# A hybrid attention layer on eight cores: value projections set among query and key projections, gates and cumulative sums moved into the projection stage

## The chip, the cores and the metric

One Trainium2 chip, eight cores. Each core runs the same program on one of the eight batch elements; no core sends anything to another. The time is the device time of the slowest core in microseconds (us). A core has a matrix engine (TensorE, PE in the rows; PEld is its weight load), a vector engine (VectorE, DVE), an activation engine (ScalarE, ACT), GpSimd (POOL) and SyncE (SP). Each engine takes its instructions strictly in program order; POOL and SP also issue DMA transfers, in the same order as their other work.

## The reference, cut

```python
hn = rms_norm(x, g_mix) * (1.0 + sc1) + sh1
proj = hn @ w_in                                  # 2048 x 3080
mq, mk, mv, fq, fk, fv, f_logit = jnp.split(proj, offs, axis=-1)   # six of 512 columns, 8 logits
mq = partial_rope(rms_norm(mq per head, moba_q_gain), positions)   # 8 heads of 64, rope on 16
mk = partial_rope(rms_norm(mk per head, moba_k_gain), positions)
fq = rms_norm(fq per head, fox_q_gain); fk = rms_norm(fk per head, fox_k_gain)
log_f = jax.nn.log_sigmoid(f_logit + b_forget)
# MoBA: blocks of 256 keys; a query keeps its own block and the top 3 past blocks
gate = einsum('bhtd,bhnd->bhtn', mq, mean of mk over each block)
# FoX: softmax(q k / 8 + cum[q] - cum[k]), cum = cumsum(log_f), causal
x = x + gt1 * (concat(o_moba, o_fox) @ w_out)
hn = rms_norm(x, g_ffn) * (1.0 + sc2) + sh2
x = x + gt2 * (swiglu(causal conv of width 3 over hn @ w_up) @ w_down)
```

## The kernel before

A sequence has 2048 tokens, 16 tiles of 128. The program is one list of operations per engine. `Prog` records each operation in program order and derives the waits from the bytes that it reads and writes, and for PSUM from the bank; the engines then run their own lists. So the order in which Python emits the work is the order on each engine, and an engine waits for its next instruction even if a later one could go.

The stages are: normalise and transpose x into `hnT` (T1), project it and prepare heads (T2), attention for 16 heads (T3), output projection and second norm (T4), the channel sub-layer (T5). The change lies in T2.

T2 works in units (line 600). A unit is one group of columns for one tile: `pe_unit(n)` does eight accumulating matmuls of 128x512 into PSUM bank `n % 4`. `groups` gives the order mq, mk, mv, fq, fk, fv, fl, each over 16 tiles: 112 units. The loop at line 674 is a software pipeline: iteration n emits `pe_unit(n)`, then `stage_a(n-1)`, `stage_b(n-4)` and `stage_a2(n-2)`.

- For mq, mk, fq and fk, `stage_a` squares the bank on ACT, sums per head on DVE (line 632) and takes the root on ACT. `stage_a2` takes the reciprocal on DVE (line 644) and multiplies the bank by it on DVE, which frees the bank.
- `stage_b` applies the gains on POOL. For mq and mk POOL first writes the 16 rope columns (128x128) and then the other 48 per head (128x384), and four DVE operations do the rope on the first product.
- For mv and fv, `stage_a` is one ACT copy from the bank and nothing else. For fl (8 columns) it is one small DVE addition.

Weights come as 512-column pieces into two alternating buffers `wch`, each piece issued by POOL when the group before it starts (line 607). Eight pieces of the adaLN weights (`late_pieces`) come through one buffer `wlate`: the transfer is issued at units 2, 14, 26, ... and PE uses the piece eight units later, the first four as 32 matmuls of one column, the last four as 8 of 512.

After the loop, lines 689 to 746 run with no projection beside them: `make_ab`; exp and log of the forget logits on ACT; two f32 matmuls that sum within and over tiles; a chain of 15 additions on DVE for the prefix over tiles; the splitting of the sum into three bf16 columns of FQ and FK; 112 one-column matmuls for the block means of the keys; and for tiles 8 to 15 the gate: eight PE transposes, a DVE copy, eight small matmuls, a DVE copy, a comparison, a reduction and the mask columns of MQ. T3 starts with POOL's memsets of `vaug` (which lies in the bytes of `hnT`), the transposes of head 0 (line 784), 16 warm-up matmuls and the first scores, whose exp is the first ACT work of T3.

Of the kernel before, what the change touches and what calls it, by code (L numbers as in the profile page):

```python
# [256 lines left out]
def build_program(debug=False, stop_after=None):  # L257
# [435 lines left out]
    act(zf, zf, AF.Ln, bias=one_ap, scale=1.0)  # L693
    ts("dve", zf, zf, -1.0, None, ALU.mult)
    pbc = pbank(4)
    mm(pbc[:, 0:128], tri_f, zf, True, True)
    pbt = pbank(5)
    mm(pbt[:, 0:128], ones_f, zf, True, True)
    copy("dve", totb, pbt[:, 0:128])
    pref3 = pref.rearrange("p (i h) -> p i h", i=NT)  # L700
    tot3 = totb.rearrange("p (i h) -> p i h", i=NT)
    memset("dve", pref3[:, 0, :], 0.0)
    for i in range(1, NT):
        tt("dve", pref3[:, i, :], pref3[:, i - 1, :], tot3[:, i - 1, :], ALU.add)
    tt("dve", cum, pbc[:, 0:128], pref, ALU.add)
    ts("dve", negcum, cum, -1.0, None, ALU.mult)
    cum3 = cum.rearrange("p (i h) -> p i h", i=NT)
    r3 = res1.rearrange("p (i h) -> p i h", i=NT)
    copy("dve", FQ[:, :, :, 64], cum3)
    tt("dve", r3, cum3, FQ[:, :, :, 64], ALU.subtract)  # L710
    copy("dve", FQ[:, :, :, 65], r3)
    tt("dve", r3, r3, FQ[:, :, :, 65], ALU.subtract)
    copy("dve", FQ[:, :, :, 66], r3)
    for q_ in range(3):
        ts("dve", FK[:, :, :, 67 + q_], FQ[:, :, :, 64 + q_], -1.0, None, ALU.mult)
# [2 lines left out]
    kmT3 = kmT.rearrange("p (h n) -> p h n", h=8)
    pbk = pbank(6)
    for h in range(H):  # L720
        for n in range(7):
            for s in range(2):
                mm(pbk[0:64, h * 8 + n: h * 8 + n + 1], MK[:, 2 * n + s, h, 0:64], invc[:, 0:1], s == 0, s == 1)
    memset("dve", kmT[0:64, :], 0.0)
    for h in range(H):
        copy("dve", kmT3[0:64, h, 0:7], pbk[0:64, h * 8: h * 8 + 7])
    for i in range(8, NT):
        b = i // 2
        sl = i % 2
        pbt_ = pbank_bf(5)  # L730
        for h in range(H):
            tr(pbt_[0:64, h * 128:(h + 1) * 128], MQ[:, i, h, 0:64], ident_b)
        copy("dve", qt0[sl][0:64], pbt_[0:64, 0:1024].rearrange("p (h q) -> p h q", h=8))
        pbg = pbank(7)
        for h in range(H):
            mm(pbg[:, h * 8:(h + 1) * 8], qt0[sl][0:64, h, :], kmT3[0:64, h, :], True, True)
        copy("dve", gate_s[sl], pbg[:, 0:64])
        g3 = gate_s[sl].rearrange("p (h n) -> p h n", h=8)
        cmp4 = cmp_s[:, 0:8 * b * b].rearrange("p (h n m) -> p h n m", h=8, n=b)
        in0 = g3[:, :, 0:b].unsqueeze(2).to_broadcast([128, 8, b, b])  # L740
        in1 = g3[:, :, 0:b].unsqueeze(3).to_broadcast([128, 8, b, b])
        tt("dve", cmp4, in0, in1, ALU.is_gt)
        rk = rank_s[:, 0:8 * b].rearrange("p (h n) -> p h n", h=8)
        P.op("dve", (lambda o, a: (lambda e: e.tensor_reduce(out=o, in_=a, axis=AX.X, op=ALU.add)))(rk, cmp4),
             reads=[cmp4], writes=[rk])
        ts("dve", MQ[:, i, :, 64:64 + b], rk, 3.0, NEG, ALU.is_ge, ALU.mult)
# [343 lines left out]
```

How the kernel before makes its waits and increments, by code:

```python
        def run_engine(ename, eng):  # L203
            seen = {}
            for o in prog.ops[ename]:
                waits = {}
                for d in o.deps:
                    key, sem, val = sem_of(d)
                    if seen.get(key, 0) >= val:
                        continue
                    if key not in waits or waits[key][1] < val:
                        waits[key] = (sem, val)
                if o.is_dma:
                    e, j = o.dma_sem
                    key = ("d", e, j)
                    pv = o.dma_val - 16
                    if pv > 0 and seen.get(key, 0) < pv:
                        if key not in waits or waits[key][1] < pv:
                            waits[key] = (dsems[e][j], pv)
                for key, (sem, val) in waits.items():
                    eng.wait_ge(sem, val)
                    seen[key] = val
                ins = o.fn(eng)
                if o.is_dma:
                    e, j = o.dma_sem
                    ins.then_inc(dsems[e][j], 16)
                elif o.signal:
                    ep = (o.sig_idx - 1) // SEM_EPOCH
                    ins.then_inc(esems[ename][ep], 1)
            if ename in dsems:
                for j, s in enumerate(dsems[ename]):
                    if dcount[ename][j] > 0:
                        eng.wait_ge(s, dcount[ename][j])
```

## Time and profile before

| | |
|---|---|
| median of 3 runs | 1477.72 us (1476.7 to 1493.68) |
| the profiled execution | 1477.1 us |
| its span, slowest core (6) | 1475.5 us; the eight cores 1465.8 to 1475.5 us |
| mean granted TensorE clock | 0.95 on each core |
| busy over the span | PE 81%, DVE 63%, ACT 51%, POOL 17% |
| chain that ended last | PE 45%, DVE 26%, issue 13%, ACT 7%, DMA 5% |

Busy shares are means over stages with different limits. A stretch of the trace shows which engine is full in it, and the idle time in brackets behind a row shows what ended the wait. The clock is given in parts of the full 2.4 GHz; 0.5 is the 1.2 GHz level, and a stretch in between is a mean over both. A matmul's time includes its way through the engine: eight in a row of 128x512 show 1.89 us, but follow one another at 1.73 us per eight.

### The profile page before, as it was taken

The page shows a single profiled execution, that of the slowest core. Times are in us where ns is not written, and L with a number is a line of the kernel's source. Part 1 is how long each engine was busy: PE and PEld are TensorE (multiplying, and loading weights), DVE is VectorE, ACT ScalarE, POOL GpSimd, SP SyncE. Part 2 cuts the span into 40 slices and gives each one's busy share as a digit, 9 for nine tenths or more (in the row PEclk, how much of TensorE's full clock was granted, in tenths as well). Part 3 has the DMA queues.
Part 4 walks back from the last instruction along what each step waited for, and adds up shares of the span by engine and source line. Part 5 has one row for each costly group of instructions (what it writes and reads, how often), then busy time and mean ns, then how long its engine had stood idle before and what let it go on. Part 6 is the DMA issues. An engine that isn't in the chain of part 4 may idle for free.

```text
span 1475.5 us, 21224 instructions; the slowest of 8 cores (1465.8 to 1475.5 us)
## 1 busy us (share of the span) xinstructions
PE 1199.8 (81%) x6516; PEld 573.3 (39%) x6516; DVE 925.6 (63%) x1420; ACT 748.8 (51%) x1212; POOL 243.9 (17%) x224
## 2 busy tenths in 40 slices
PE   0086569995799999889999894589997989989888
PEld 0052224444444444434444343434443434434333
DVE  3508883726466666666666535578748865875885
ACT  1062223330488888768888402567416732751770
POOL 1014440331000000230000000023202320330330
PEclk9999999995799999989999996899999999999999
DMA  9851345430000001110000440122112112121105
GB/s 226 160 67 28 49 61 83 70 46 2 1 1 2 1 1 30 44 44 1 1 1 15 123 149 1 34 67 43 30 58 57 29 29 72 29 43 43 30 15 228
DMA packets 34557, 74.32 MB, mean 50 GB/s; under 512 B 2960, under 2 KB 21392, under 8 KB 34320
## 3 DMA queue, kind: packets, MB, share of 16 engines
q0 software_dynamic: 22928, 30.43, 14.3%
q1 hardware_dynamic: 11520, 42.54, 8.7%
q8 instruction: 56, 0.92, 0.3%
q14 instruction: 53, 0.43, 0.1%
HBM read 94.99 MB, written 8.39 MB: 70 GB/s over the span
## 4 chain that ended last, share of the span: by engine, by line
PE 45%; DVE 26%; issue 13%; ACT 7%; DMA 5%; another core or an unknown queue 2%; DVEq 1%; POOL 1%; ACTq 0%; POOLq 0%; SPq 0%
PE psum L467 39%; DVE arena L457 10%; DVE arena L439 8%; ACT arena L436 6%; PE psum L471 6%; DVE arena L461 4%; DMA arena<-w_ada 2%; DMA arena<-w_down 2%; DVE arena L632 2%; DVE arena L553 1%; DVE arena L448 1%; DMA arena<-w_in 1%; DVEq L221 1%; DVE arena L644 0%
## 5 line engine op out<-in xcount | busy, mean ns | idle before, releaser
L467 PE MATMUL psum<-arena 128*128 128x512 bf16 (+12 forms) x5428 | 1108.6, 348 | 207.3 <-DMA arena<-w_ada 70.4
L467 PEld LDWEIGHTS psum<-arena 128*128 128x128 bf16 (+5 forms) x5428 | 464.9, 101 | 727.0 <-issue 321.5
L436 ACT ACTIVATE arena<-psum,arena 128x512 bf16<-128x512 f32 x704 | 408.9, 642 | 134.9 <-PE psum L467 106.3
L436 ACT ACTIVATE arena<-arena 128x1024 f32<-128x1024 f32 (+2 forms) x319 | 193.6, 633 | 278.6 <-DVE arena L632 78.7
L457 DVE SCALAR_TENSOR_TENSOR arena<-arena 128x1024 f32<-128x1024 f32 x176 | 264.1, 1520 | 62.5 <-ACT arena L436 53.3
L439 POOL TENSOR_TENSOR arena<-arena 128x1024 bf16<-128x1024 f32 (+3 forms) x132 | 189.5, 1446 | 580.3 <-DVE arena L457 485.6
L439 DVE TENSOR_TENSOR arena<-psum,arena 128x1024 f32<-128x1024 f32 (+4 forms) x173 | 148.5, 862 | 171.3 <-PE psum L467 161.7
L436 ACT ACTIVATE arena<-psum 128x1024 f32<-128x1024 f32 (+2 forms) x184 | 146.4, 796 | 187.9 <-PE psum L467 178.8
L439 DVE TENSOR_TENSOR arena<-arena 128x4 f32<-128x4 f32 (+5 forms) x370 | 184.3, 520 | 57.0 <-DMA arena<-w_down 24.5
L471 PE MATMUL psum<-arena 1*128 1x1 f32 (+4 forms) x1088 | 160.0, 255 | 63.8 <-DVE arena L461 25.7
L471 PEld LDWEIGHTS psum<-arena 1*128 1x128 f32 (+4 forms) x1088 | 120.6, 139 | 170.2 <-issue 158.9
L461 DVE COPY arena<-psum 64x512 f32<-64x512 f32 (+3 forms) x209 | 138.5, 665 | 73.7 <-PE psum L471 41.4
L461 POOL COPY arena<-arena 128x1024 bf16<-128x1024 bf16 x16 | 16.6, 1041 | 400.1 <-PE psum L467 400.1
L439 DVE TENSOR_TENSOR arena<-arena,psum 64x512 bf16<-64x512 f32 x64 | 43.9, 686 | 59.5 <-PE psum L467 59.0
L632 DVE TENSOR_REDUCE arena<-arena 128x8 f32<-128x512 f32 x64 | 43.6, 681 | 42.6 <-ACT arena L436 39.8
L436 ACT ACT_TABLE_LOAD x5 | 6.4, 1283 | 87.7 <-DVE arena L553 71.6
L553 DVE SCALAR_TENSOR_TENSOR arena<-arena 128x1024 bf16<-128x1024 f32 x32 | 39.0, 1219 | 13.6 <-DMA arena<-x 13.6
L448 DVE TENSOR_SCALAR arena<-arena 128x1024 f32<-128x1024 f32 (+4 forms) x41 | 28.1, 686 | 5.8 <-DVE arena L557 2.6
L461 DVE CAST arena<-arena 128x4 bf16<-128x4 f32 (+2 forms) x69 | 18.7, 272 | 14.8 <-ACT arena L436 7.5
L464 POOL MEMSET arena<- 128x16 bf16 (+7 forms) x26 | 7.4, 354 | 106.6 <-PE psum L467 87.6
L867 DVE RECIPROCAL arena<-psum 128x4 f32<-128x4 f32 x64 | 11.3, 176 | 18.9 <-PE psum L471 18.6
L474 POOL DMA_DIRECT2D arena<-w_up x22 | 13.0, 593 | 56.6 <-DVE arena L439 56.6
(16 smaller groups left out, 47.1 us busy)
## 6 DMA issues: line engine op xcount, KB each, us to landing
arena<-x SPq DMA_DIRECT2D x32, 512.0 KB, 22.4
arena<-w_ada POOLq DMA_DIRECT2D x12, 1024.0 KB, 12.7
arena<-w_up POOLq DMA_DIRECT2D x22, 512.0 KB, 5.2
arena<-w_down SPq DMA_DIRECT2D x22, 512.0 KB, 4.0
out<-arena SPq DMA_DIRECT2D x16, 512.0 KB, 2.7
arena<-w_in POOLq DMA_DIRECT2D x6, 1024.0 KB, 10.4
arena<-w_out SPq DMA_DIRECT2D x8, 512.0 KB, 3.6
arena<-bcastb SPq DMA_DIRECT2D x1, 1024.0 KB, 9.0
```

What stands on the lines that cost most here:

```text
L221: eng.wait_ge(sem, val)
L436: return P.op("act", lambda e: e.activation(out=out, in_=in_, func=func, **kw), reads=rd, writes=wr)
L439: return P.op(eng, lambda e: e.tensor_tensor(out=out, in0=in0, in1=in1, op=op), reads=[in0, in1], writes=[out])
L448: return P.op(eng, lambda e: e.tensor_scalar(out=out, in0=in0, scalar1=s1, scalar2=None, op0=op0), reads=rd, writes=[out])
L457: return P.op(eng, lambda e: e.scalar_tensor_tensor(out=out, in0=in0, scalar=scalar, in1=in1, op0=op0, op1=op1), reads=rd, writes=[out])
L461: return P.op(eng, lambda e: e.tensor_copy(out=out, in_=in_), reads=[in_], writes=[out])
L467: return P.op("pe", lambda e: e.matmul(out, lhsT=lhsT, rhs=rhs, start=start, stop=stop), reads=[lhsT, rhs], writes=[out])
L471: return P.op("pe", lambda e: e.transpose(out=out, in_=in_, identity=ident), reads=[in_, ident], writes=[out])
L474: return P.dma(eng, lambda e: e.dma_start(out=out, in_=in_), reads=[in_], writes=[out])
L553: P.op("dve", (lambda o, a, acc: (lambda e: e.scalar_tensor_tensor(out=o, in0=a, scalar=1.0, in1=a, op0=ALU.mult, op1=ALU.mult, accum_out= ...
L632: P.op("dve", (lambda o, a: (lambda e: e.tensor_reduce(out=o, in_=a, axis=AX.X, op=ALU.add)))(ss8[sl], sq_s[sl].rearrange("p (h d) -> p h ...
L867: P.op("dve", (lambda o, a: (lambda e: e.reciprocal(out=o, in_=a)))(rcol[nb], pcol), reads=[pcol], writes=[rcol[nb]])
```

## The change

- The units are reordered, and the fl units go: 96 units. mq and mk units come in order, and from the fourth on each of the next 16 is followed by one mv unit. The order is mq0 to mq3, mv0, mq4, mv1, ..., mq15, mv12, mk0, mv13, mk1, mv14, mk2, mv15, mk3 to mk15 (unit 47), then fq (48 to 63), fk (64 to 79), fv (80 to 95).
- Small buffers that alternated with the unit number now alternate with `slot`, which counts only the units that use them.
- mv's weights have a buffer of their own, `wmv`, in the bytes of FV (not written before unit 80), which overlap the last x tiles of T1. The fl weights have a small buffer `wfl`. POOL issues mq, mv, fl at the start of T2 and mk at unit 0; fq's piece is issued at mk0, fk's at fq0, fv's at fk0.
- The work after the loop is cut into parts, and a table `extra_at` emits each at the end of an iteration: fl matmuls of a tile at 33 to 48 into bank 7; block means at 39 to 51 into bank 6; their copy and one addition for all fl tiles at 54; gates of tiles 8 to 15 at 80 to 95, a transposing half at even and the rest at odd iterations; the cumulative sum at 83, 85, 88 and 91.

```diff
-    groups = ["mq", "mk", "mv", "fq", "fk", "fv", "fl"]
-    units = [(gi, gname, i) for gi, gname in enumerate(groups) for i in range(NT)]
+    units = []
+    for j_ in range(32):
+        units.append((0, "mq" if j_ < NT else "mk", j_ % NT))
+        if 3 <= j_ < 3 + NT:
+            units.append((0, "mv", j_ - 3))
+    units += [(0, g_, i_) for g_ in ("fq", "fk", "fv") for i_ in range(NT)]
+    slot, c_ = [], 0
+    for _, g_, _ in units:
+        slot.append(c_)
+        c_ += g_ in ("mq", "mk", "fq", "fk")
+    wmv = sb(MV_O + NT * 512 * 2, 8 * 512, BF16).rearrange("p (k c) -> p k c", k=8)
     dma("pool", wch[0], win_v[:, :, 0:512])
+    dma("pool", wmv, win_v[:, :, 1024:1536])
+    dma("pool", wfl, win_v[:, :, 3072:3080])
+    big = ["mq", "mk", "fq", "fk", "fv"]
     def pe_unit(n):
-        if i == 0 and gi + 1 < len(groups):
...
+        bi_ = big.index(gname) if gname != "mv" else -1
+        if i == 0 and 0 <= bi_ and bi_ + 1 < len(big):
+            c0_ = gcol[big[bi_ + 1]]
+            dma("pool", wch[(bi_ + 1) % 2], win_v[:, :, c0_:c0_ + 512])
+        wb = wch[bi_ % 2] if gname != "mv" else wmv
...
-        sl = n % 2
+        sl = slot[n] % 2
...
+    def cum_part(part):
+        if part == -1:
+            act(zf, zf, AF.Exp, scale=-1.0)
+            act(zf, zf, AF.Ln, bias=one_ap, scale=1.0)
+            ts("dve", zf, zf, -1.0, None, ALU.mult)
+        elif part == 0:
+            mm(pbc, tri_f, zf, True, True)
+            mm(pbt, ones_f, zf, True, True)
+            copy("dve", totb, pbt)
+            memset("dve", pref3[:, 0, :], 0.0)
+            for i in range(1, 8):
+                tt("dve", pref3[:, i, :], pref3[:, i - 1, :], tot3[:, i - 1, :], ALU.add)
+        elif part == 1:
+            for i in range(8, NT):
+                tt("dve", pref3[:, i, :], pref3[:, i - 1, :], tot3[:, i - 1, :], ALU.add)
+            tt("dve", cum, pbank(6)[:, 0:128], pref, ALU.add)
+            ts("dve", negcum, cum, -1.0, None, ALU.mult)
+        else:
...
+    def kmean_part(n_):
...
+    def kmean_out():
+        memset("dve", kmT[0:64, :], 0.0)
+        copy("dve", kmT3[0:64, :, 0:7], pbank(6)[0:64, 0:64].rearrange("p (h n) -> p h n", h=8)[:, :, 0:7])
+    def fl_tile(i):
+        for k in range(8):
+            mm(pbank(7)[:, i * 8:(i + 1) * 8], hnT[:, k, i * 128:(i + 1) * 128], wfl[:, k, :], k == 0, k == 7)
+    def fl_out():
+        tt("dve", zf3, pbank(7)[:, 0:128].rearrange("p (i h) -> p i h", i=NT),
+           smalls[:, S_BF:S_BF + 8].unsqueeze(1).to_broadcast([128, NT, 8]), ALU.add)
+    def gate_head(i):
+        for h in range(H):
+            tr(pbt_[0:64, h * 128:(h + 1) * 128], MQ[:, i, h, 0:64], ident_b)
+        copy("dve", qt0[sl][0:64], pbt_[0:64, 0:1024].rearrange("p (h q) -> p h q", h=8))
+    def gate_rest(i):
+        for h in range(H):
+            mm(pbg[:, h * 8:(h + 1) * 8], qt0[sl][0:64, h, :], kmT3[0:64, h, :], True, True)
+        copy("dve", gate_s[sl], pbg[:, 0:64])
...
+    for i_ in range(NT):
+        at(33 + i_, fl_tile, i_)
+    for b_ in range(7):
+        at(39 + 2 * b_, kmean_part, b_)
+    at(54, kmean_out)
+    at(54, fl_out)
+    for i_ in range(8, NT):
+        at(80 + 2 * (i_ - 8), gate_head, i_)
+        at(81 + 2 * (i_ - 8), gate_rest, i_)
+    at(83, cum_part, -1)
+    at(85, cum_part, 0)
+    at(88, cum_part, 1)
+    at(91, cum_part, 2)
     for n in range(NU + 4):
...
             stage_a2(n - 2)
+        for f_ in extra_at.get(n, []):
+            f_()
     make_ab(ab2, S_GFFN, 4, 3)
-    act(zf, zf, AF.Exp, scale=-1.0)
...
```

## Rows read from the trace of the kernel before

**Rows 1.** Stretches: length; busy us (count) of PE, PEld, DVE, ACT, POOL; clock; DMA.
```profile
103.00:214.00 111.00, 67.72 (x336) 27.11 (x336) 92.42 (x212) 26.54 (x66) 47.63 (x64) 0.97 0.38 53
214.00:333.00 119.00, 116.76 (x614) 52.91 (x615) 55.51 (x118) 42.76 (x94) 30.36 (x28) 1.00 0.45 65
333.00:337.00 4.00, 3.38 (x113) 3.14 (x109) 2.25 (x15) 0.32 (x1) 0.05 (x1) 1.00 0.02 6
337.00:381.00 44.00, 21.66 (x275) 19.03 (x276) 27.50 (x85) 1.99 (x3) 4.13 (x6) 0.51 0.00 1
381.00:387.00 6.00, 6.00 (x23) 2.46 (x22) 0.69 (x1) 0.00 (x0) 0.00 (x0) 0.64 0.00 0
```
**Rows 2.** Timeline, PE: start, length, line, operands, count [idle time before, releaser].
```profile
103.10 13.33 PE L467 MATMUL psum<-arena 128*128 128x512 bf16 x48 [4.01 <-DMA arena<-w_in]
...
138.52 1.89 PE L467 MATMUL psum<-arena 128*128 128x512 bf16 x8 [1.61 <-DVE arena L439]
...
214.59 48.52 PE L467 MATMUL psum<-arena 128*128 128x512 bf16 x280 [1.63 <-DVE arena L439]
```
**Rows 3.** Timeline, DVE and POOL, one mq unit after its multiply.
```profile
138.29 0.68 DVE L632 TENSOR_REDUCE arena<-arena 128x8 f32<-128x512 f32 x1
138.58 0.46 POOL L439 TENSOR_TENSOR arena<-arena 128x128 f32<-128x128 f32 x1 [1.99 <-DVE arena L439]
138.88 0.30 DVE L439 TENSOR_TENSOR arena<-arena 128x128 f32<-128x128 f32 x1
138.99 1.05 POOL L439 TENSOR_TENSOR arena<-arena 128x384 bf16<-128x384 f32 x1
139.11 1.02 DVE L439 TENSOR_TENSOR arena<-arena 128x64 f32<-128x64 f32 x1
140.23 0.23 DVE L439 TENSOR_TENSOR arena<-arena 128x64 f32<-128x64 f32 x1
```
**Rows 4.** Timeline: mk15's multiply, ACT's first square of fq, a reciprocal of fq.
```profile
216.43 0.69 DVE L439 TENSOR_TENSOR arena<-psum,arena 128x512 f32<-128x512 f32 x1
...
242.55 0.60 ACT L436 ACTIVATE arena<-psum 128x512 f32<-128x512 f32 x1 [1.18 <-PE psum L467]
...
247.31 0.19 DVE L644 RECIPROCAL arena<-arena 128x8 f32<-128x8 f32 x1
```
**Rows 5.** Timeline from fv's last copy to the first exp of attention.
```profile
332.72 0.60 ACT L436 ACTIVATE arena<-psum 128x512 bf16<-128x512 f32 x1 [2.86 <-PE psum L467]
...
342.33 3.96 DVE L439 TENSOR_TENSOR arena<-arena 128x8 f32<-128x8 f32 x15
...
349.64 1.55 DVE L448 TENSOR_SCALAR arena<-arena 128x128 bf16<-128x128 bf16 x3 [0.17 <-DVE arena L461]
...
354.09 0.35 PE L467 MATMUL psum<-arena 64*128 64x8 bf16 x8 [5.33 <-DVE arena L461]
...
372.45 0.68 DVE L461 COPY arena<-psum 64x1024 bf16<-64x1024 bf16 x1
...
373.28 0.35 PE L467 MATMUL psum<-arena 64*128 64x8 bf16 x8 [1.72 <-DVE arena L461]
...
375.41 0.19 DVE L450 TENSOR_SCALAR arena<-arena 128x56 bf16<-128x56 f32 x1
...
387.19 1.16 ACT L436 ACTIVATE arena<-psum,arena 128x512 bf16<-128x512 f32 x2 [47.70 <-PE psum L467]
```
**Rows 6.** Groups of PE transposes: in attention (400:830), then in the stretch 337:387.
```profile
L471 PE MATMUL psum<-arena 128*72 128x128 bf16 x216 | 20.8, 219 | 4.3 <-DVE arena L461 4.0
L471 PE MATMUL psum<-arena 128*64 128x128 bf16 x64 | 8.5, 314 | 0.0
```
**Rows 7.** T1's transposes on PE; POOL's issues of mq and mk, landing times of three.
```profile
74.27 21.37 PE L471 MATMUL psum<-arena 128*128 128x128 f32 x128
...
91.31 1.74 POOL L474 DMA_DIRECT2D arena<-w_in  x2
...
DMA to landing us min/median/max: 11.5/18.2/22.9
```

More of the change, by code:

```diff
@@ L368, in build_program @@
     wlate = sb(A.take(8 * 512 * 2), 8 * 512, BF16).rearrange("p (k c) -> p k c", k=8)
+    wfl = sb(A.take(8 * 8 * 2), 64, BF16).rearrange("p (k c) -> p k c", k=8)
     t2_end = A.p
@@ L641, in stage_a2 @@
         pb = pbank(n % 4)
-        sl = n % 2
+        sl = slot[n] % 2
         pb3 = pb.rearrange("p (h d) -> p h d", h=8)
@@ L672, in stage_b @@
         tt("dve", dst[:, i, :, 0:16], a3, b3, ALU.add)
+    def cum_part(part):
+        cum3 = cum.rearrange("p (i h) -> p i h", i=NT)
+        r3 = res1.rearrange("p (i h) -> p i h", i=NT)
+        pref3 = pref.rearrange("p (i h) -> p i h", i=NT)
+        tot3 = totb.rearrange("p (i h) -> p i h", i=NT)
+        if part == -1:
[3 more added lines that the diff above has]
+        elif part == 0:
+            pbc = pbank(6)[:, 0:128]
+            pbt = pbank(6)[:, 128:256]
+            mm(pbc, tri_f, zf, True, True)
[10 more added lines that the diff above has]
+        else:
+            copy("dve", FQ[:, :, :, 64], cum3)
+            tt("dve", r3, cum3, FQ[:, :, :, 64], ALU.subtract)
+            copy("dve", FQ[:, :, :, 65], r3)
+            tt("dve", r3, r3, FQ[:, :, :, 65], ALU.subtract)
+            copy("dve", FQ[:, :, :, 66], r3)
+            for q_ in range(3):
+                ts("dve", FK[:, :, :, 67 + q_], FQ[:, :, :, 64 + q_], -1.0, None, ALU.mult)
@@ new lines, in build_program @@
+    kmT3 = kmT.rearrange("p (h n) -> p h n", h=8)
+    def kmean_part(n_):
+        pbk = pbank(6)
+        for h in range(H):
+            for s_ in range(2):
+                mm(pbk[0:64, h * 8 + n_: h * 8 + n_ + 1], MK[:, 2 * n_ + s_, h, 0:64], invc[:, 0:1], s_ == 0, s_ == 1)
+    def kmean_out():
[4 more added lines that the diff above has]
+            mm(pbank(7)[:, i * 8:(i + 1) * 8], hnT[:, k, i * 128:(i + 1) * 128], wfl[:, k, :], k == 0, k == 7)
@@ new lines, in fl_out @@
+    def fl_out():
+        tt("dve", zf3, pbank(7)[:, 0:128].rearrange("p (i h) -> p i h", i=NT),
+           smalls[:, S_BF:S_BF + 8].unsqueeze(1).to_broadcast([128, NT, 8]), ALU.add)
+    def gate_head(i):
+        sl = i % 2
+        pbt_ = pbank_bf(5)
+        for h in range(H):
+            tr(pbt_[0:64, h * 128:(h + 1) * 128], MQ[:, i, h, 0:64], ident_b)
+        copy("dve", qt0[sl][0:64], pbt_[0:64, 0:1024].rearrange("p (h q) -> p h q", h=8))
+    def gate_rest(i):
+        b = i // 2
+        sl = i % 2
+        pbg = pbank(7)
+        for h in range(H):
+            mm(pbg[:, h * 8:(h + 1) * 8], qt0[sl][0:64, h, :], kmT3[0:64, h, :], True, True)
+        copy("dve", gate_s[sl], pbg[:, 0:64])
+        g3 = gate_s[sl].rearrange("p (h n) -> p h n", h=8)
+        cmp4 = cmp_s[:, 0:8 * b * b].rearrange("p (h n m) -> p h n m", h=8, n=b)
+        in0 = g3[:, :, 0:b].unsqueeze(2).to_broadcast([128, 8, b, b])
+        in1 = g3[:, :, 0:b].unsqueeze(3).to_broadcast([128, 8, b, b])
+        tt("dve", cmp4, in0, in1, ALU.is_gt)
+        rk = rank_s[:, 0:8 * b].rearrange("p (h n) -> p h n", h=8)
+        P.op("dve", (lambda o, a: (lambda e: e.tensor_reduce(out=o, in_=a, axis=AX.X, op=ALU.add)))(rk, cmp4),
+             reads=[cmp4], writes=[rk])
+        ts("dve", MQ[:, i, :, 64:64 + b], rk, 3.0, NEG, ALU.is_ge, ALU.mult)
@@ L674, in build_program, with at @@
+    extra_at = {}
+    def at(n_, f_, *a_):
+        extra_at.setdefault(n_, []).append(lambda: f_(*a_))
+    for i_ in range(NT):
[11 more added lines that the diff above has]
+    at(91, cum_part, 2)
     for n in range(NU + 4):
@@ L691, in build_program @@
     dump("gtb", gtb, [128, 2048])
-    act(zf, zf, AF.Exp, scale=-1.0)
[L693 to L715, printed above, removed]
@@ L716, in build_program @@
-    dump("cum", cum, [128, 128])
[L718 to L746, printed above, removed]
```

14 lines of the change are left out of this document (5 added, 9 removed).

## The prediction

> **What bounds the kernel now.** I read the page first (PE busy 81% of the span, DVE 63%), then the chain of waits, then the stretches of the projection stage, since the change touches that stage alone. [rows 1] cuts it: 111 us for mq and mk, 119 for mv, fq, fk and fv, 4 for fl, and 44 in which no projection runs but gates, cumulative sums and the first head's transposes; then 6 us of warm-up matmuls. Look there at two columns. In the first stretch DVE is busy 92 of 111 us and PE 68, so DVE sets the pace; from 214 to 333 it is PE, 117 of 119 us. In the 44 us tail neither is full, PE's granted clock is 0.51 (its 1.2 GHz level), and ACT has 2 us of work: a latency chain.
>
> [rows 2] shows the pace of the first stretch: each unit's eight matmuls wait 1.6 us for the DVE multiply that frees their bank. From 138.52 (unit 12) to 214.59 (unit 34) are 22 units, 3.458 us each. From 214.59 on PE runs without a break; the 48 us row is 27 units at 1.726 and two ada pieces of 0.95. That is the opening: mq/mk leave PE 1.6 to 1.7 us per unit, and an mv unit costs 1.726 and no DVE work.
>
> **The change, part by part.**
>
> *mv between mq and mk.* Sixteen pairs each get one PE-only unit. PE needs 2 x 1.726 = 3.45 per pair, DVE 3.458 as before, so the pair should stay on DVE's pace. One thing in DVE's loop gets tighter. The order of DVE is reduce(m), rope(p), reciprocal(m), multiply(m); today the rope is that of two mq/mk units back, and with mv in every second place, it is the unit multiplied just before. So the rope now waits for POOL's first product of the same tile. In [rows 3] POOL starts 0.2 us after the multiply's end (138.37), ends its short product at 139.04 and goes straight into the 1.05 us one, to 140.04. The first rope operation starts at 138.88 today, and could then start at about 139.2 at the earliest. Yet the second one, issued 0.1 us after POOL's long product, takes 1.02 us where its twin takes 0.23 at 140.23: it is held until POOL is done. So rope already ends on POOL's end. If the first operation slips in beside POOL the delay is 0; if it is held as the second is, its 0.30 us falls behind 140.04, less the overlap of neighbours, some 0.2; if every step simply shifts, 0.32, and with both effects 0.5. I take 0.2 (the nearest row is an operation of the same kind that was held): 16 x 0.2 = 3.2 us, ends 0 and 8. The Trainium skill (SBUF — State Buffer, Who interferes with whom) says that a DVE instruction with two SBUF inputs and a GpSimd one that reads SBUF exclude each other for a whole instruction, whichever started first. The 1.02 us row agrees, and by that rule the full 0.30 would be paid, 4.8 us in place of 3.2.
>
> PE has two ada pieces (0.95 each) in the pairs with 0.2 us of slack per pair: 1.0 us lost.
>
> Now the join. mk15's multiply ends at 217.1 today [rows 4]; with the reduce of fq0, which now stands before it, 217.7, plus 3.2 makes 220.9. DVE then still has the ropes of mk14 and mk15 among fq units: multiplies of fq0, fq1, fq2 end at 224.4, 227.8, 229.4. Unit fq6 needs fq2's bank, so it starts at 229.5, and from there fq is PE's pace again (1.73 a unit; DVE's part there, reduce 0.68, reciprocal 0.19 and multiply 0.69 [rows 3, 4], is 1.6). Today fq0's matmuls end at 242.45, where ACT takes them, so fq6 starts at 242.45 + 5 x 1.726 = 251.1. **Gain: 251.1 - 229.5 - 1.0 = 20.6 us** (16 to 24).
>
> *Weight loads.* POOL issues mq, mv, fl, mk in that order. wmv lies over the last x tiles, so its issue waits for the transposes' end at 95.6 (mq's goes at 91.3 as before), and behind it wait fl's and mk's loads, the first ada piece and POOL's products, which come only after the first units' multiplies. Today mq, mk and ada land 11.5, 18.2 + 92.2 = 110.4 and 22.9 + 93.0 = 115.9 [rows 7]. mv takes mk's place: about 110.4, as the queue is busy with mq until 102.8 anyway. PE reaches unit 4 at 103.10 + 13.33 less two units, 113.0 [rows 2]: 2.6 us of slack, no cost; each us later than 113 would cost one. The piece behind mk lands some 6 us later than today, at 122; PE wants it after unit 10, behind mq4's multiply at about 125. fq's load (at mk0) waits for mq15's matmuls, done by then. Later loads keep their units. Cost 0.
>
> *fl and kmean between mk units.* fl is 128 matmuls of 8 columns, today 113 of them in 3.38 us [rows 1], 30 ns each: 0.24 per tile, and 16 small ones per kmean part under 0.9; mk units leave PE 1.7 us each. Cover: PE's wait for DVE; without it 4 + 6 us. The sixteen DVE adds become one in fq. **fl's stage is gone: it lies inside the tail below.**
>
> *Gates and sums among the fv units.* fv needs no DVE, so DVE has some 30 us there. A gate tile today takes from 354.09 to 373.28 for seven, 2.74 us each, all in series [rows 5], so less than that of DVE; two fv units and PE's part give 4.4. The DVE chain hides. PE does not: eight transposes at 96 to 133 ns [rows 6] and eight matmuls at 30 ns make 1.0 to 1.3 per tile; at the full clock, which fv has, 1.0, so 8.0 in all, and the two sum matmuls 0.6: 8.6 us. Beside this, the sum's steps stand in DVE's queue before the next tile's copy, on which PE then waits in order. The scan's 15 adds took 3.96 and are cut in two with room to spare; the last piece (what lies between 346.3 and 351.2 less two operations that go with the part before, about 4.2) comes at unit 91, after tile 13's own 2.0 (as tile 15's, 373.63 to 375.60) and before tile 14's copy of 0.7: 6.9 us, while PE has 1.73 + 0.75 + 1.73 = 4.2 to do. Stall 2.7 (0 to 5). ACT's exp and log, 2 us with their table load [rows 1], lie beside copies of 0.60 in units of 1.73.
>
> **Sum.** fv's last unit ends at 332.6 today [rows 5]; new: 332.6 - 20.6 + 8.6 + 2.7 = 323.3 for the end of the last gate matmuls. Those end at 373.63 today, and from there to the first exp of attention, 387.19, is 13.6 us of the same work in the same order (tile 15's gate, four transposes with copies, 16 warm-up matmuls). I add 0.7: make_ab and 4 us of POOL's memsets and copies, today early in the tail [rows 1], now fall into that chain (0 to 1.6). Against it, warm-up took 6 us at clock 0.64 [rows 1] and would take 3.5 at 1.0; PE is mostly idle for 8 us before it, as it was when the clock was low, so I count nothing (0 to -2.9). First exp: 323.3 + 13.6 + 0.7 = 337.6 against 387.2, **49.6 us earlier**. Nothing behind it is tied to absolute time: attention's loads are issued by step, and its code is unchanged. From the profiled execution's 1477.1 us (span 1475.5, 1.6 around it; the median of the runs, 1477.72, is 0.6 higher): **1427.5 us**. The ends taken together (loop 0 to 8, PE's part 8.6 to 11, stall 0 to 5, ada pieces hidden or not, tail) give 1416 to 1438.
>
> **Rivals.**
> *The cover in fv fails.* DVE's queue, in order, puts each tile's chain and the sums in PE's way. If every tile still cost its 2.74 and the scan its 9 us (342.3 to 351.2), the 11.3 us become 22 + 9 = 31: 1447. For it: PE waits in order; today it waits 1.72 us ahead of tile 15's matmuls [rows 5]. Against: two units of 1.73 stand between copy and matmul.
> *The pair runs in series.* If mv's matmuls add to the loop (a bank, or ACT's in-order square behind mv's copy), 16 x 1.73 = 27.6 us stand in place of 4.2: 1451. Against: ACT is busy 27 of 111 us, and PE's wait in [rows 2] is nearly as long as an mv unit.
> *Slower: the clock.* If PE, with waits of 2 us no longer between units but gate work instead, is granted its 1.2 GHz level from fq to fv, a unit costs twice 1.73, 48 x 1.73 = 83 us more: 1510. It decides from 29 units on at that level. For it: 0.51 in the tail, with such small matmuls. Against: 1.00 from 214 to 333 with PE 98% busy, and 0.97 in the first stretch with a wait in each unit.
> *Better than the sum:* warm clock in the tail, no stall, no loop delay: below 1416.
>
> **Chances.** The forecast (1416 to 1438) 0.71, the cover 0.11, the series 0.10, below 1416 0.04, the clock 0.04. A range from 1416 to 1446 holds the first and about half of the cover's case (costs are partial as a rule): 8 in 10. A measurement of this kernel tells about 2% from no change, which is 1448.2: faster takes the forecast, the better case, and three fifths of cover and series together, 0.87; same 0.09; slower 0.04.
>
> **What the new profile would show.** Right: no stretch of 1.2 GHz between 110 us and the last fv unit; multiplies of mq/mk 3.6 to 3.7 us apart while mv runs, 3.46 after; fq6 at about 230; PE's idle time ahead of gate matmuls only near unit 93; first exp near 337. Wrong: PE waiting on arena<-w_in at unit 4 (mv too late); pairs of 5 us (series); gate matmuls each waiting for a DVE copy (cover); a PE clock of 0.5 in fv. If the stage ends at 337 and the time is not near 1427, attention has changed its pace, which nothing here predicts.

## The result, and the profile after

| | before | after |
|---|---|---|
| median of the runs, us | 1478.22 (15 runs) | 1440.35 (12 runs) |
| profiled execution, us (its longest span) | 1477.1 (1475.5) | 1445.49 (1443.9) |
| first w_in matmul to first exp of attention, mean over the 8 cores, us | 282.2 | 234.7 |
| the same, core 6 | 284.1 | 232.9 |

The ratio of after to before is 0.9717, 95% interval [0.9684, 0.975]: faster, by 37.9 us where 50 were forecast. On two other chips the same kernel took 1432.08 (ratio 0.9682) and 1429.91 us (0.9671). The comparisons leave out executions in which one die took over 1% longer than the other at a lower clock, or that took over 1.5% longer than the kernel's fastest; of the twelve after the change that is two.

So two things have to be explained: a stage that became 47.5 us shorter, 2 less than forecast, and some 10 us by which the first chip's median gained less than the stage.

*The stage.* Stretches of core 6: pairs, mk alone, fq to fv, tail. Columns as in [rows 1].

```profile
102.92:188.82 85.90, 82.31 (x536) 38.30 (x537) 64.55 (x158) 29.55 (x65) 34.78 (x48) 0.97 0.61 84
188.82:226.31 37.49, 25.80 (x256) 13.95 (x257) 33.30 (x79) 8.63 (x22) 16.45 (x22) 1.00 0.42 57
226.31:321.00 94.69, 90.82 (x509) 40.84 (x509) 67.57 (x160) 33.37 (x76) 24.73 (x21) 1.00 0.31 45
321.00:336.00 15.00, 8.73 (x56) 4.98 (x54) 6.24 (x11) 0.63 (x2) 3.42 (x6) 0.77 0.00 1
```

Against [rows 1], PE is now full where DVE had set the pace (82 of 86 us), the 44 us with neither full have become 15, and the clock is 0.97 to 1.00 up to the end of fv.

Timeline of PE on core 6, as [rows 2]: start, length, line, operands, count [idle time before, releaser].

```profile
124.16 60.96 PE L468 MATMUL psum<-arena 128*128 128x512 bf16 x432 [0.97 <-DVE arena L440]
...
220.23 2.48 PE L468 MATMUL psum<-arena 128*128 128x512 bf16 x24 [1.57 <-DVE arena L440]
...
226.31 14.08 PE L468 MATMUL psum<-arena 128*128 128x512 bf16 x64 [0.74 <-DVE arena L440]
...
280.31 0.63 PE L472 MATMUL psum<-arena 128*64 128x128 bf16 x8
...
286.55 0.63 PE L472 MATMUL psum<-arena 128*64 128x128 bf16 x8
287.12 4.02 PE L468 MATMUL psum<-arena 128*128 128x512 bf16 x24
...
314.46 3.90 PE L468 MATMUL psum<-arena 64*128 64x8 bf16 x24 [2.34 <-DVE arena L462]
318.29 0.63 PE L472 MATMUL psum<-arena 128*64 128x128 bf16 x8
318.86 2.19 PE L468 MATMUL psum<-arena 128*128 128x512 bf16 x16
...
326.00 0.61 PE L472 MATMUL psum<-arena 128*72 128x128 bf16 x8 [4.39 <-DVE arena L462]
```

The 1.6 us waits of [rows 2] are gone while mv runs: one row of 61 us without a break. Behind 280.31 one gate tile comes every two units, and the only wait for DVE among them is the 2.34 us at 314.46. The last gate matmuls end at 321.05 (318.86 + 2.19).

Timeline of DVE and POOL in a pair, as [rows 3], then the first exp.

```profile
142.22 0.68 DVE L645 TENSOR_REDUCE arena<-arena 128x8 f32<-128x512 f32 x1
142.93 1.01 POOL L440 TENSOR_TENSOR arena<-arena 128x384 bf16<-128x384 f32 x1
143.08 1.00 DVE L440 TENSOR_TENSOR arena<-arena 128x128 f32<-128x128 f32 x1 [0.18 <-POOL arena L440]
144.00 0.21 DVE L440 TENSOR_TENSOR arena<-arena 128x64 f32<-128x64 f32 x1
...
145.23 0.69 DVE L440 TENSOR_TENSOR arena<-psum,arena 128x512 f32<-128x512 f32 x1
...
335.82 1.84 ACT L437 ACTIVATE arena<-psum,arena 128x512 bf16<-128x512 f32 x4 [14.37 <-PE psum L468]
```

The first rope operation now waits 0.18 us for POOL's short product, starts behind the start of the long one and takes 1.00 us where it took 0.30 in [rows 3]; the second takes 0.21 where it took 1.02. The multiply comes 3.61 us after the one before it (141.62): 0.15 over 3.458.

*What is not in the stage.* Span and mean granted clock of each core in the profiled execution:

```profile
core 0: 1420.5 us, clock 0.961
core 1: 1426.4 us, clock 0.956
core 2: 1443.7 us, clock 0.939
core 3: 1443.9 us, clock 0.942
...
core 6: 1424.7 us, clock 0.961
```

Six cores end where the sum put the slowest, or earlier (1427.5 less 1.6 around the span is 1425.9); cores 2 and 3 end 18 us later. Some 4 us of that they have at the first exp already (340.53 and 341.52, where core 6 has 335.82). From there to their end they take 1103.2 and 1102.4 us, the other six 1088.0 to 1089.7, and the eight cores of the kernel before 1086.8 to 1088.3. So what follows the stage is within some 1 us as long as before, but for 14 us on two cores, and these have one place. Timeline of PE on cores 2 and 3, one row each:

```profile
1065.40 26.81 PE L468 MATMUL psum<-arena 128*128 128x512 bf16 x99 [6.90 <-ACT arena L437]
...
1066.72 25.63 PE L468 MATMUL psum<-arena 128*128 128x512 bf16 x96 [6.71 <-ACT arena L437]
```

Stretches of core 2, and behind the last "..." two of core 3 (the granted clock is the third number from the end):

```profile
1070.00:1074.00 4.00, 4.00 (x20) 1.83 (x19) 3.05 (x3) 3.09 (x4) 0.58 (x1) 1.00 0.00 0
1074.00:1078.00 4.00, 4.00 (x18) 1.70 (x16) 3.47 (x2) 2.68 (x4) 2.31 (x2) 0.85 0.27 22
1078.00:1082.00 4.00, 3.91 (x16) 1.63 (x15) 2.73 (x3) 3.42 (x5) 0.95 (x1) 0.81 0.55 110
...
1230.00:1234.00 4.00, 4.00 (x16) 1.63 (x15) 3.61 (x3) 2.53 (x4) 0.06 (x1) 0.81 0.75 125
1234.00:1238.00 4.00, 4.00 (x18) 1.77 (x17) 2.91 (x2) 3.25 (x4) 2.28 (x1) 0.89 0.00 0
...
1074.00:1078.00 4.00, 4.00 (x17) 1.65 (x16) 2.73 (x2) 3.67 (x5) 2.90 (x2) 0.84 0.00 0
1078.00:1082.00 4.00, 4.00 (x17) 1.69 (x16) 3.79 (x4) 2.37 (x4) 0.00 (x0) 0.81 0.74 129
```

Both cores come out of a 7 us wait at a boundary between two groups of the channel sub-layer, as the other cores do, in code that the change does not touch. They run at 1.00 for a few us, then at 0.81 from about 1075 to 1236, both over the same stretch: a spell, in what follows. Over 1078:1234 the other six have 0.97 to 0.99. Seven of the first chip's ten compared executions had such a pair of neighbouring cores (0/1, 2/3, 4/5 or 6/7; lowest mean clock 0.939 to 0.942) and took 1439.5 to 1445.5 us, and so had the two left out (0.925 and 0.937); the three others took 1427.44, 1427.51 and 1430.72.

### The profile page after: what moved, and what is told of

Read it like the earlier page. It is cut to its first block, busy times and chain, and to the rows that moved or that the text cites. A ratio compares the mean times of both kernels' runs of the same rounds, so it can differ in the third digit from the quotient of the medians.

```text
span 1443.9 us, 21154 instructions; the slowest of 8 cores (1420.4 to 1443.9 us)
## 1 busy us (share of the span) xinstructions
PE 1217.6 (84%) x6516; PEld 574.4 (40%) x6516; DVE 918.2 (64%) x1398; ACT 748.0 (52%) x1212; POOL 242.4 (17%) x224
## 4 chain that ended last, share of the span: by engine, by line
PE 54%; DVE 21%; issue 10%; DMA 6%; ACT 5%; another core or an unknown queue 2%; POOL 1%; DVEq 0%; ACTq 0%; POOLq 0%; SPq 0%
PE psum L468 48%; DVE arena L458 7%; DVE arena L440 6%; PE psum L472 6%; ACT arena L437 5%; DVE arena L462 4%; DMA arena<-w_ada 2%; DMA arena<-w_down 2%; DVE arena L554 1%; DMA arena<-w_in 1%; DVE arena L449 1%; DVE arena L645 1%; POOL arena L440 0%; DVEq L221 0%
## 5 line engine op out<-in xcount | busy, mean ns | idle before, releaser
L468 PE MATMUL psum<-arena 128*128 128x512 bf16 (+12 forms) x5428 | 1130.4, 353 | 156.2 <-DMA arena<-w_ada 73.0
L440 DVE TENSOR_TENSOR arena<-arena 128x4 f32<-128x4 f32 (+6 forms) x370 | 180.3, 509 | 59.5 <-DMA arena<-w_down 24.8
L472 PE MATMUL psum<-arena 1*128 1x1 f32 (+4 forms) x1088 | 156.4, 249 | 65.6 <-DVE arena L462 28.5
L472 PEld LDWEIGHTS psum<-arena 1*128 1x128 f32 (+4 forms) x1088 | 117.7, 135 | 175.0 <-issue 163.7
L554 DVE SCALAR_TENSOR_TENSOR arena<-arena 128x1024 bf16<-128x1024 f32 x32 | 39.0, 1220 | 9.4 <-DMA arena<-x 9.4
L924 DVE RECIPROCAL arena<-psum 128x4 f32<-128x4 f32 x64 | 11.3, 177 | 20.0 <-PE psum L472 19.8
```

Of the source, the lines that this page charges most:

```text
L440: return P.op(eng, lambda e: e.tensor_tensor(out=out, in0=in0, in1=in1, op=op), reads=[in0, in1], writes=[out])
L468: return P.op("pe", lambda e: e.matmul(out, lhsT=lhsT, rhs=rhs, start=start, stop=stop), reads=[lhsT, rhs], writes=[out])
L472: return P.op("pe", lambda e: e.transpose(out=out, in_=in_, identity=ident), reads=[in_, ident], writes=[out])
L554: P.op("dve", (lambda o, a, acc: (lambda e: e.scalar_tensor_tensor(out=o, in0=a, scalar=1.0, in1=a, op0=ALU.mult, op1=ALU.mult, accum_out= ...
L924: P.op("dve", (lambda o, a: (lambda e: e.reciprocal(out=o, in_=a)))(rcol[nb], pcol), reads=[pcol], writes=[rcol[nb]])
```

## The experiments

Two theories stood after the traces. Of the stage: the gain is the two parts of the change, as summed. Of the rest: the spells at 0.81 come either from a less idle TensorE earlier on (history: 44 us at 1.2 GHz are gone), or from both cores of a pair coming out of the gap at a group boundary close together (coincidence). The first four ran on a second chip.

**again**: the changed kernel, unchanged.

> The changed kernel again, unaltered, as the measure for the other three. Its profiled execution had cores 2 and 3 at a granted clock of 0.81 from 1075 to 1235 us, beginning 4 us after both had resumed dense matmuls from an idle gap, within 1.3 us of each other; undisturbed executions took 1427 us, those with such a pair about 1440. All theories: again about two in three executions with at least one pair of neighbouring cores at a mean clock under 0.946, 12 to 16 us above the rest; lowest near 1427, median near 1440.

1432.08 us (1429.13 to 1434.96), ratio 0.9682 [0.9663, 0.9702]. The spells are there, but short. Stretches of core 4, which had left a 6.87 us wait at 1063.56, then one of core 5, which had left 6.75 us at 1065.10:

```profile
1076.00:1080.00 4.00, 4.00 (x19) 1.73 (x18) 2.90 (x3) 3.25 (x4) 0.78 (x1) 0.91 0.57 111
1080.00:1084.00 4.00, 4.00 (x17) 1.69 (x16) 3.63 (x3) 2.53 (x4) 1.57 (x1) 0.81 0.02 4
...
1092.00:1096.00 4.00, 4.00 (x19) 1.79 (x18) 2.31 (x3) 3.26 (x5) 1.41 (x1) 0.95 0.41 82
...
1088.00:1092.00 4.00, 4.00 (x17) 1.66 (x16) 2.63 (x3) 2.91 (x4) 2.90 (x2) 0.81 0.00 0
```

Some 15 us at 0.81 on both, and as long again at about 1220 and 1340, behind each of three group boundaries. But not only there: core 4 has 15 us at about 796, in the output projection, and at 937. The first of these, where ACT does nothing and DVE little:

```profile
796.00:811.00 15.00, 15.00 (x59) 6.28 (x58) 4.31 (x4) 0.00 (x0) 0.00 (x0) 0.82 0.96 300
```

The same kernel runs at 0.81 for 160 us in one spell on one chip, and for 15 us five times on another. From the first exp to the end cores 4 and 5 take 1094.8 and 1094.5 us here, the other six 1087.3 to 1089.1: a cost of 6 us, where the long spell cost 14.

**idle**: 166 dependent small DVE operations ahead of attention bring back an idle stretch of 44 us.

```
     dump("cum", cum, [128, 128])
+    for _ in range(166):
+        tt("dve", rank_s[:, 0:8], rank_s[:, 0:8], rank_s[:, 0:8], ALU.min)
```

> The changed kernel with 166 dependent small DVE operations (about 44 us) ahead of attention, so that PE rests there as it did before the change. Theory of history (the low clock comes because PE no longer rests at 340 to 380 us): the disturbed pairs go, median and lowest near 1471. Theory of coincidence (two neighbouring cores step from idle to dense matmuls at the same moment in the channel sub-layer; the change brought the cores of a pair closer together): a delay that is the same on each core alters nothing, about two in three executions disturbed, lowest near 1471, median near 1484.

1475.14 us (lowest 1471.74): 43.1 over again, about the idle time itself, and cores with mean clocks down to 0.930 stay; in the profiled execution core 4 is at 0.81 over 981:996. A rest ahead of attention does not keep the spells away: the theory of history falls.

**t5_after, t5_again, t5_before**: in the channel sub-layer each w_down load and its scaling, until then in one block at a group's start, comes after the first half of its unit; in the changed kernel on two chips, and in the kernel before.

```
-        for ml in range(gs):
-            st_ = stage5[scnt5 % 2]
-            ...
-            tt("dve", wdnb[:, ml, :], st_, gtb[:, 1024:2048], ALU.mult)
...
                 ucnt += 1
+                if half == 0:
+                    st_ = stage5[scnt5 % 2]
+                    ...
+                    tt("dve", wdnb[:, ml, :], st_, gtb[:, 1024:2048], ALU.mult)
```

> The changed kernel with the loads and scalings of w_down spread over the units of a group, one behind each first half, in place of all of them ahead of the group. The block of DVE scalings at a group's start goes, and with it the idle gap of PE of about 7 us at each of the four groups. Theory of coincidence: without the gaps there is no step, few or no disturbed pairs; 4 gaps of 4 to 7 us saved, 1400 to 1412, lowest and median close together. Theory of history or of density: PE is denser still, as many disturbed pairs or more; lowest 1400 to 1412, median 12 us or more above it.

> The changed kernel with the channel sub-layer's weight loads spread, once more, as the partner of t5_gap on the same chip. It gave 1420.6 with no disturbed pair in four executions. If the gap at the group boundary is the cause, there is again none or nearly none, and the time is 1419 to 1423; if the earlier run was luck, pairs at a lower clock appear in half of the executions and the median is 1425 or more.

> The kernel before with the same edit of the channel sub-layer alone. Both theories: the gaps' 16 to 28 us saved, 1450 to 1462, few disturbed pairs. If the saving here is as large as on the changed kernel, the edit and the change add up.

t5_after 1420.6 us (ratio 0.9606 [0.9588, 0.9623]), t5_again 1420.13 (0.9614 [0.96, 0.9628]), t5_before 1469.43 (0.9946 [0.9922, 0.9971]). PE on core 3 of t5_after, where the other runs have a gap of 7 us:

```profile
1069.85 7.07 PE L468 MATMUL psum<-arena 128*128 128x512 bf16 x32 [1.02 <-DMA arena<-w_up]
1077.80 7.07 PE L468 MATMUL psum<-arena 128*128 128x512 bf16 x32 [0.88 <-ACT arena L437]
```

No gap, and a pause of about 1 us in every 8. In the eight compared executions of the two runs no core's mean clock is under 0.963. But most of the 11.5 us under again are the gaps' own time. From the first exp to the end, cores without any spell take 1078.6 to 1079.0 us in t5_after (0 to 3) and 1087.3 and 1088.6 in again (6 and 7), 8 to 10 us; and in the kernel before the same edit saves 10.4 (1479.81 to 1469.43 on that chip). The forecasts of 1400 to 1412 and 1450 to 1462 were too low: a gap of 7 us gave back less than its length, as the short pauses stand in its place.

And the gap is not needed for a spell: t5_before has no such gap either, and in its profiled execution (1486.4 us; mean clock 0.927 to 0.928 on cores 0 to 3, 0.951 to 0.957 on the others) cores 2 and 3 fall to 0.81 at about 1232 and stay there, but for some 7 us before 1258, to the end. Cores 0 and 1 have theirs earlier, until about 300, in the projection stage, which takes 297.1 and 298.1 us on them and 280.2 to 283.2 on the others. On core 2, then core 3, then core 0:

```profile
1230.00:1240.00 10.00, 10.00 (x41) 4.22 (x40) 8.08 (x6) 6.41 (x10) 3.02 (x1) 0.84 0.10 22
1300.00:1310.00 10.00, 10.00 (x40) 4.16 (x39) 9.24 (x7) 6.32 (x9) 3.13 (x1) 0.81 0.26 69
...
1300.00:1310.00 10.00, 10.00 (x40) 4.16 (x39) 8.64 (x6) 6.21 (x8) 4.00 (x3) 0.81 0.47 99
...
102.00:200.00 98.00, 66.91 (x296) 25.24 (x301) 86.08 (x198) 23.07 (x58) 44.33 (x60) 0.81 0.30 44
222.00:242.00 20.00, 19.80 (x105) 8.78 (x106) 0.82 (x2) 5.37 (x9) 1.74 (x2) 0.81 0.07 7
```

On cores 2 and 3 PE is busy 10.00 of 10 us, as in the spells above (4.00 of 4, or nearly). On core 0 it is not: among the mq and mk units it is busy 66.9 of 98 us. And among the mv units, where PE is full, DVE and ACT have little to do. So neither a PE without pauses nor other busy engines are a condition of a spell.

**t5_gap**: t5_again with the gap put back, without loads.

```
     for g, gs in enumerate(GSZ):
+        if g > 0:
+            for _ in range(53):
+                tt("dve", ss_a[:, 0:8], ss_a[:, 0:8], ss_a[:, 0:8], ALU.min)
```

> The changed kernel with the channel sub-layer's weight loads spread (as t5_after), plus 53 dependent small VectorE operations (14 us) at the start of each group but the first, which holds VectorE as the block of weight scalings did and makes TensorE wait some 7 us and resume, without any load. Theory of the gap (both cores of a pair resume at full rate from a long gap at about the same moment, and the chip then grants them 0.81): pairs of neighbouring cores at a clock some 0.02 under the others come back in most executions, and the time goes from 1420.6 to 1428 or more, beyond the gaps' own cost. Rival (the queue of loads ahead of the groups, not the gap, brings it): no such pair, and the time is 1420.6 plus the gaps alone.

1445.26 us (1444.25 to 1446.79). Timeline of PE on core 4, then core 5:

```profile
1060.97 19.24 PE L468 MATMUL psum<-arena 128*128 128x512 bf16 x73 [7.15 <-ACT arena L437]
...
1055.29 15.60 PE L468 MATMUL psum<-arena 128*128 128x512 bf16 x64 [7.16 <-ACT arena L437]
1071.75 8.61 PE L468 MATMUL psum<-arena 128*128 128x512 bf16 x34 [0.86 <-DMA arena<-w_up]
```

One stretch of each, behind these rows:

```profile
1072.00:1076.00 4.00, 4.00 (x16) 1.63 (x15) 3.79 (x4) 2.44 (x4) 0.61 (x2) 0.81 0.71 108
...
1072.00:1076.00 4.00, 4.00 (x17) 1.69 (x16) 3.76 (x3) 2.98 (x4) 2.79 (x1) 0.81 0.43 122
```

Short spells (some 6 us) are back behind the gaps, so a gap helps to bring them. But of the 25.1 us the three gaps of 7.15 are already 21.5, and the spells cost nothing that shows: from the first exp to the end cores 0 to 3, which have none, take 1105.0 to 1106.2 us, and cores 4 to 7, which have them, 1105.9 to 1106.0. And cores 4 and 5 left the gap 5.7 us apart and fell together all the same: how close they resume does not decide, nor does a short pause (0.86 us on core 5) just ahead. Of the coincidence only this is left: the fall takes both cores of a pair at once.

**inter and tail**: one part of the change each. inter has the interleaved mv units, with fl, sums and gates as stages behind; tail has the old order of units (mq, mk, mv, fq, fk, fv), with fl, kmean, sums and gates inside units. Both edits are shown, cut, against the changed kernel; inter also drops the table of parts and puts the old lines back behind the loop.

```
inter:
-    units += [(0, g_, i_) for g_ in ("fq", "fk", "fv") for i_ in range(NT)]
+    units += [(0, g_, i_) for g_ in ("fq", "fk", "fv", "fl") for i_ in range(NT)]
tail:
-    for j_ in range(32):
-        ...
+    units = [(0, g_, i_) for g_ in groups for i_ in range(NT)]
```

> The change's first part alone: mv units between mq and mk units with their weights loaded early; fl as a stage of 16 units, cumulative sums, kmean and gates behind it in series, as before. The prediction's sum gives 251.1 - 229.5 - 1.0 = 20.6 us for this part, and the rest is as before: 1478 - 20.6 = 1457 us, ratio 0.986. In its profile the last fv unit should end near 312 and the first exp come near 366. If the profile's reading is wrong and the pair runs in series (5.2 us a pair), the time stays within 5 us of before. If the parts help each other (tail work needs the room that interleaving makes), this part is worth less than 15 us alone.

> The change's second part alone: units in the old order (mq, mk, mv, fq, fk, fv), fl, kmean, sums and gates moved into units, no tail. By the prediction's terms the stage of fl and tail goes from 332.6..387.2 = 54.6 us to 14.3, less 8.6 of PE work among the fv units and 2.3 to 2.7 of stall, so 29 us earlier: about 1449, ratio 0.980. In this order the fl and kmean units 33 to 54 fall into mv and fq, where PE sets the pace, so 16 x 0.24 + 7 x 0.5 = 7 us more may have to be paid: 1456 then. If both parts add up, the gains of inter and tail make 47 to 51 us together.

inter took 1456.21 us, ratio 0.9855 [0.9838, 0.9873], its stage 21.0 us shorter than before (261.2, mean over the cores); tail 1459.83, 0.9882 [0.9865, 0.9898], its stage 19.0 shorter (263.2), where 1449 was forecast, or 1456 with fl and kmean uncovered. Together 40.0; both in one kernel give 47.5. The missing 7.5 us stand in one row of tail, PE on core 7 from mv on:

```profile
216.43 56.20 PE L468 MATMUL psum<-arena 128*128 128x512 bf16 x512 [1.45 <-DVE arena L440]
```

[rows 2] has 48.52 us there: 7.7 us more for 120 of the 128 fl matmuls and the 112 kmean matmuls, which fall among units where PE sets the pace. That is the prediction's "without it 4 + 6 us", sized: the interleaving pays a second time, because it makes mk units the place with room for fl.

**late**: mv's units begin after mq 6 instead of mq 3, and each late ada piece is used two units later.

```
-        if 3 <= j_ < 3 + NT:
-            units.append((0, "mv", j_ - 3))
+        if 6 <= j_ < 6 + NT:
+            units.append((0, "mv", j_ - 6))
...
-        if n % 12 == 10 and n // 12 < len(late_pieces):
-            sg, hf = late_pieces[n // 12]
+        if n % 12 == 0 and 0 <= n // 12 - 1 < len(late_pieces):
+            sg, hf = late_pieces[n // 12 - 1]
```

> The changed kernel with mv's units beginning three mq units later (after mq 6 in place of mq 3) and each late piece of the ada weights used two units later. On the early core of a pair TensorE waited 1.3 us for mv's weights (unit 4) and 3.4 us for the first ada piece (unit 10); both waits should go, and on those cores the stage ends 1.3 to 3.4 us earlier. On the late core of each pair, which sets the time, nothing was waited for: the time stays within 1.5 us of again2 if the lost distance between the cores of a pair does not matter. If it is that lost distance which brings the spells at 0.81 (theory of coincidence), disturbed pairs become rarer and the time is up to 4 us under again2.

It was meant for two waits that the changed kernel shows on other cores than core 6, here on core 2 at the first ada piece and on core 5 at unit 4:

```profile
127.44 7.80 PE L468 MATMUL psum<-arena 128*128 128x1 bf16 x50 [3.39 <-DMA arena<-w_ada]
...
106.33 5.34 PE L468 MATMUL psum<-arena 128*128 128x512 bf16 x24 [1.42 <-DMA arena<-w_in]
```

In late no core waits for either, yet it took 1433.7 us beside 1429.91 for again2, a difference inside the intervals, and its stage is 236.2 us against 233.4. The pairs now last until unit 43, and fl and kmean, still from unit 33 on, fall among them: on core 0 unit 53 starts 128.0 us after the first w_in matmul (230.11 less 102.07), in again2 123.5 (224.85 less 101.31). That is the cover again, taken away for some ten units. It hides whatever the weight waits gave, and the lost distance within a pair was not isolated by it.

**split, best, again2**: the sum's last piece cut in three, that with the spread loads, and the changed kernel beside them on a third chip.

```
-    at(91, cum_part, 2)
+    at(89, cum_part, 2)
+    at(91, cum_part, 3)
+    at(93, cum_part, 4)
```

> The changed kernel with the sum's last piece (three copies, two subtractions, three negations into the added columns, 4.2 us of VectorE) cut into three, after units 89, 91 and 93, where it stood whole after unit 91. The prediction's stall (2.7 us; 2.34 in the trace) came from that piece standing ahead of tile 14's copy. If that is its cause, the 2.3 us wait ahead of the gate matmuls of unit 93 goes, three smaller ones of 0 to 0.5 stand in its place, and the first exp comes some 1.5 to 2.3 us earlier: time 1.5 to 2.3 us under again2. If the wait was set by the gate tile's own chain of copies, it stays and the time does not move.

> The changed kernel with the channel sub-layer's weight loads spread (t5_after, 1420.1 and 1420.6) and the sum's last piece in three (split). If both add up, 1418 to 1419 us, ratio 0.960.

> The changed kernel unchanged, partner of split and late on the same chip. By the sum of the prediction 1427.5 where no pair of cores has a spell at granted clock 0.81; 1432 as in the run before (again) with spells of some 13 us; 1440 or more with spells of over 100 us.

split took 1428.83 us and again2 1429.91, too near to tell apart by the time; the trace does tell. Timeline of PE on core 6 of split:

```profile
310.56 2.17 PE L468 MATMUL psum<-arena 64*128 64x8 bf16 x16 [0.73 <-DVE arena L462]
312.66 0.63 PE L472 MATMUL psum<-arena 128*64 128x128 bf16 x8
313.23 5.74 PE L468 MATMUL psum<-arena 128*128 128x512 bf16 x32
```

The wait of 2.34 us is one of 0.73, and the stage 1.1 us shorter (232.3 against 233.4), a little under the 1.5 forecast. best took 1417.17 us (1415.8 to 1417.89), ratio 0.9583 [0.9566, 0.9601], and is faster than both kernels.

## Why the prediction was right, step by step

*The forecast time and its sum.* 1427.5 us is about what the changed kernel takes where no long spell occurs (1427.44, 1427.51 and 1430.72 on the first chip; medians 1432.08 and 1429.91 on the others). The first chip's median, 1440.35, lies 13 us above and inside the range 1416 to 1446. That it does is luck: the forecast proper was 1416 to 1438, and what the range had beyond it was meant for the cover's failing, which did not happen. Some of the 1427.5 is luck as well: the stage became 51.2 us shorter on core 6 and 47.5 on the mean of the eight where 49.6 were summed, and the terms below miss by up to 2.3 us, in both directions. The step that did not hold is "nothing behind it is tied to absolute time: attention's loads are issued by step, and its code is unchanged". The code was indeed unchanged, and on six cores the time from the first exp to the end was so within some 1 us, but the sum let the clock stay as in the profile of before, which has no spell. Nor was it attention that changed its pace, as the prediction's last sentence has it: the long spell lies in the channel sub-layer. Spells were no new thing, as t5_before shows with the stage as it was. Why the first chip has longer ones than the other two, and what brings them, stays open.

*mv between mq and mk.* Forecast 20.6; the part alone brought 21.0 in the stage and 21.5 in the time. On core 6, 226.31 is unit 53 (the rows from there to 280.31 hold 240 matmuls, thirty eights: units 53 to 80 and two ada pieces of gate columns), so fq6, unit 54, starts at 228.04 where 229.5 stood. With the start 0.18 earlier (102.92 for 103.10), and the 1.0 for two ada pieces, which the sum charged behind fq6, that is 2.3 us better than summed. 0.8 of it is the loop: 16 x 0.15 in place of 16 x 0.2. The rest, the ada pieces and the join, the rows do not separate. The case that came is the one taken, the first rope operation held as the second had been, and it cost 0.15 where 0.2 was taken: behind the held operation now stands one more, of 0.21, less the overlap of neighbours. As the prediction read the Trainium skill (SBUF — State Buffer, Who interferes with whom), the full 0.30 would have been paid. The exclusion itself agrees beside POOL's long product (1.00 us for the operation that starts there), though [rows 3] has 0.30 beside the short one; but only one operation a pair is held, now as before, and what was paid is the change from the second to the first.

*Weight loads at no cost.* True on core 6. On cores 5 and 7, which reached unit 4 before their pair's other core, PE waited 1.42 and 1.28 us for mv, and on cores 2, 5 and 7 it waited 3.39, 1.49 and 0.93 for the first ada piece; core 0, as early, waited for neither. The prediction read its slack (2.6 us; 122 against 125) off core 6, whose first units had run slowly (13.33 us in [rows 2], where cores that start early have 10.52). An early core has that much less slack. A late one is not safe either: in again core 6 began 5 us behind core 7 and waited 1.33 us at unit 4.

*fl and kmean between mk units.* Nothing there, as forecast; uncovered it is 7.7 us (tail), inside the "4 + 6".

*Gates and sums among the fv units.* 8.6 + 2.7 forecast. A tile of two units comes at 4.51 us (286.55 to 291.06 with the row 287.12 in it), 1.06 over two units. From fv0's end (280.31) to the last gate matmuls (321.05) are 40.7 us; fifteen units (25.9), two ada pieces of gate columns (eight matmuls of 512 columns like a unit's, so 1.72) and the 11.3 make 40.65. The sum is right by terms that miss in both directions. PE's part was 9.0 in place of 8.6 (eight times 1.06, and 0.54 for the sums, in whose tile 5.05 us pass, from 291.06 to 296.11). In it the transposes were under their price (0.57 a tile from one start to the next row's, 71 ns each, where attention, at a clock of 0.98, had given 96 and the tail, at 0.51, 133) and the gate matmuls over it (0.49 a tile in place of 0.24). The stall was 2.34. split shows the stall's cause to be the one named: the sum's last piece in DVE's queue ahead of tile 14's copy.

*The tail.* 14.3 forecast, 14.8 measured (321.05 to 335.82). The added 0.7 became more: the chain's DVE operations run beside POOL's copies, and PE waits 4.39 us for them at 326.00. The row that begins with the warm-up (330.35, 22 matmuls) took 5.77 us where it had 6.35 before, the clock being 0.72 over 330:336 in place of 0.65; so to count nothing for a warmer clock was about right.

*The rivals.* The cover failed nowhere (one wait of DVE among the gates), the pair was no series (3.61 us, not 5.2), and no stretch from fq to fv fell to 1.2 GHz (1.00). The loss came at a third level, 0.81, on two cores and in a stage that no rival covered.

## What to carry to other kernels

Give an engine's slack a place: work moved under a wait is free only while that wait is there, so size both parts of such a change together (40.0 us apart, 47.5 together). Read the slack of a load on every core, the earliest above all, and the time on the latest. And where a sum ends at "the rest is unchanged", look at the granted clock of every core in the rest before giving the range.

## What the runs showed of the hardware that was not expected

TensorE's granted clock had a level of 0.81 beside 1.00 and 0.5, and it took both cores of one neighbouring pair at once, for some 6 us (t5_gap), 15 (again) or 160 and more (after, t5_before). The Trainium skill (TensorE: Matmul & The Clock Gate, Part 1) describes a 13/16 limit, which is 0.81, on a whole die; the level agrees, but in these rows it is on two cores of a die while the other two have 0.97 and 0.99. A spell is not costly by itself: those of 6 us cost nothing that shows, five of 15 us cost 6 us, one of 160 us cost 14.

What brings a spell did not come out. In the channel sub-layer short ones stood behind gaps of 7 us, after which both PEs ran with hardly a pause, and in the eight compared executions with a pause of 1 us in every 8 no core's mean clock was under 0.963. But a PE that hardly pauses is not enough: fq to fv ran at 1.00 on core 6 with PE busy 90.8 of 94.7 us. It is not needed either: t5_before was at 0.81 among the mq and mk units with PE busy 66.9 of 98 us. And it does not hang on the other engines: 0.81 was there with DVE and ACT nearly idle (again at 796, t5_before at 222).
